# Where twenty-nine modulation tiles are read, and which engine makes the value blocks' low parts, in a two-layer diffusion backbone

## The reference, cut to what matters

```python
def even_project(u, w_in, ...):
    z = (u @ w_in).astype(jnp.float32)
    gq, gk, gv, gg, ga, mq, mk, mv, mo, mg = jnp.split(z, splits, axis=-1)
    ...
    if rope_gla is not None:                      # latent tokens only
        gq, gk = apply_rope(gq, *rope_gla), apply_rope(gk, *rope_gla)
        mq, mk = apply_rope(mq, *rope_ml), apply_rope(mk, *rope_ml)
    log_a = (jax.nn.log_sigmoid(a_pre) / GLA_TAU)...
    ...
def apply_rope(x, cos, sin):
    x1, x2 = x[..., :half], x[..., half:]
    return jnp.concatenate([x1 * c - x2 * s, x1 * s + x2 * c], axis=-1)
...
    m_lat = (jax.nn.silu(c) @ mod_w[layer] + mod_b[layer])[:, None, :]     # mod_w[layer]: 1024 x 6144
    sh1, sc1, g1, sh2, sc2, g2 = jnp.split(m_lat, 6, axis=-1)
```

## Time and profile before

| | |
|---|---|
| time, median of 3 runs | 1694.23 us (1692.0 to 1694.25) |
| the profiled execution's own time | 1690.38 us, of which the profile's span is 1688.6 us |
| TensorE matmuls busy | 1642.8 us, 97% of the span |
| VectorE / ScalarE / GpSimd busy | 1128.0 / 898.9 / 674.4 us |
| mean granted TensorE clock | 0.991 of full speed |
| weights loaded by SyncE | 281 transfers of 512 KB |

### The profile page before, as it was taken

One profiled execution on the slowest core, in us unless ns is written; L12 is line 12 of the kernel. 1 busy time (PEld: TensorE's weight loads), 2 busy tenths in 40 slices (PEclk: granted clock), 3 DMA queues, 4 the chain that ended last, 5 costly groups with the idle time before them and its releaser, 6 DMA issues.

```text
span 1688.6 us, 27407 instructions
## 1 busy us (share of the span) xinstructions
PE 1642.8 (97%) x10094; PEld 1451.7 (86%) x10094; DVE 1128.0 (67%) x1807; ACT 898.9 (53%) x1529; POOL 674.4 (40%) x494
## 2 busy tenths in 40 slices
PE   8999999998999999999999999999999999999997
PEld 5777888887899999999888889987668989998886
DVE  4678866667978888888657664145773778886113
ACT  5682435776565556665333453214883557776332
POOL 1233225453234444443443533342005266665444
PEclk9999999999999999999999999999999999999998
DMA  9423224343212223233733333364214123223221
GB/s 360 152 87 125 77 76 150 102 142 123 76 59 76 94 91 103 88 98 111 279 129 120 125 113 125 125 220 151 86 58 149 51 89 110 98 100 106 94 94 63
DMA packets 71240, 197.43 MB, mean 117 GB/s; under 512 B 6322, under 2 KB 27186, under 8 KB 69826
## 3 DMA queue, kind: packets, MB, share of 16 engines
q1 hardware_dynamic: 49268, 177.29, 30.1%
q10 hardware_dynamic: 21840, 18.40, 3.7%
HBM read 187.22 MB, written 8.45 MB: 116 GB/s over the span
## 4 chain that ended last, share of the span: by engine, by line
PE 68%; DVE 15%; ACT 5%; issue 2%; DMA 2%; POOL 2%; ACTq 0%; DVEq 0%; SPq 0%; POOLq 0%
PE ps L3824 19%; PE ps L3959 7%; PE ps L3319 6%; PE ps L4027 6%; PE ps L3446 5%; PE ps L3332 4%; PE ps L3956 3%; PE ps L3318 2%; PE ps L3774 2%; DMA raw<-in_weights 2%; PE ps L4127 2%; PE ps L4140 2%; PE ps L4106 2%; PE ps L3897 2%; PE ps L3452 1%
## 5 line engine op out<-in xcount | busy, mean ns | idle before, releaser
L895 POOL TENSOR_TENSOR wsp<-raw,wsp 128x512 fp32r<-128x512 f32 x220 | 326.6, 1505 | 691.4 <-ACT wsp L1048 691.0
L1048 ACT ACTIVATE wsp<-raw 128x1024 fp32r<-128x1024 f32 x110 | 116.7, 1061 | 169.5 <-PE ps L3319 84.2
L3959 PE MATMUL ps<-hsp,wsp 128*128 128x512 f32 x456 | 154.6, 391 | 0.0
L3824 PE MATMUL ps<-T,wun 128*128 128x384 f32 (+1 forms) x792 | 148.6, 340 | 3.9 <-DVE ps L2225 3.1
L3824 PEld LDWEIGHTS ps<-T,wun 128*128 128x128 f32 x792 | 141.4, 190 | 4.6 <-issue 4.5
L3332 PE MATMUL ps<-wsp,u 128*128 128x512 f32 x576 | 133.2, 391 | 2.6 <-POOL wsp L895 1.3
L3332 PEld LDWEIGHTS ps<-wsp,u 128*128 128x128 f32 x576 | 107.5, 188 | 28.0 <-POOL wsp L895 2.3
L3319 PE MATMUL ps<-u,wsp 128*128 128x512 f32 (+1 forms) x384 | 125.3, 362 | 0.0
L3446 PE MATMUL ps<-u,wsp 128*128 128x512 f32 x384 | 122.8, 402 | 0.0
L3956 PE MATMUL ps<-hsp,wsp 128*128 128x256 f32 x432 | 119.8, 281 | 2.6 <-DVE hsp L2821 2.1
L4027 PE MATMUL ps<-hsp,wsp 128*128 128x512 f32 x480 | 110.9, 390 | 1.8 <-POOL wsp L895 1.8
(11 more groups left out here) (412 smaller groups left out, 3866.8 us busy)
## 6 DMA issues: line engine op xcount, KB each, us to landing
raw<-in_weights SPq DMA_DIRECT2D x281, 512.0 KB, 3.3
nab<-in_nabias ACTq DMA_DIRECT2D x32, 256.0 KB, 2.7
start_w<-in_start SPq DMA_DIRECT2D x6, 1024.0 KB, 19.8
hidden_scratch<-hid0a SPq DMA_DIRECT2D x16, 384.0 KB, 4.7
hid0a<-hidden_scratch SPq DMA_DIRECT2D x5, 768.0 KB, 6.8
h<-in_x SPq DMA_DIRECT2D x4, 768.0 KB, 7.8
mD<-rows_scratch ACTq DMA_DIRECT2D x12, 256.0 KB, 3.9
mqs<-rows_scratch ACTq DMA_DIRECT2D x12, 256.0 KB, 4.8
```

Of the source, the lines that this page charges most:

```text
L895: pool.tensor_tensor(w[:, 1, half], raw[:, raw_index(s) % 4, half], w[:, 0, half].bitcast(F32), ALU.subtract)\
L1048: act.activation(split_of(s)[:, 0, :], raw[:, raw_s % 4, :], ACT.Copy).then_inc(*own.one(hi_ready))
L3824: mm = pe.matmul(out, UNIT[x][:, wp, tile(i)], operand[:, i, xp, 0:out.shape[-1]], start=(start and i == 0 and a == 0), stop=(i == KH - 1 ...
L3959: mm = pe.matmul(lat_of(layer, g, mm_), w, hsp[:, kk, xp, LAT], start=one, stop=last, skip_group_check=True)
```

## The change

Four modulation tiles leave the value blocks. After the change value blocks 5 to 8 have none, every later block up to 28 does a tile with a lower number than before, and blocks 22, 24, 26 and 28 (`TWO_MODS`) do two. The load order follows: w4, m4, w5, w6, w7, w8, w9, m5, w10, m6, w11, ... w20, m16, w21, m17, w22, m18, m19, w23, m20, w24, m21, m22, w25, m23, w26, m24, m25, w27, m26, w28, m27, m28, w29.

`value_low(b)` makes value block b's low part on VectorE, in one instruction over 1024 elements; GpSimd passes over those eight blocks. For n = 1 to 4 VectorE makes half of the rotated copy (two copies of 32 partitions), ScalarE the other half.

```diff
+TWO_MODS = [s_feat(n) for n in (14, 16, 18, 20)]
+def mods_of(s):
+    if S_V <= s < S_V + 4:
+        return []
+    first = s if s < S_V else s - 4 + sum(x < s for x in TWO_MODS)
+    return range(first, first + 1 + (s in TWO_MODS))
...
-        order += [("w", s)] + ([("m", MOD_FIRST + s)] if s < S_OUT0 else
+        order += [("w", s)] + ([("m", MOD_FIRST + x) for x in mods_of(s)] if s < S_OUT0 else
...
-            for s in range(N_START, s_feat(P2_FIRST) + 2):
+            for s in range(N_START, S_V):
+                low(s, 0)
+            lo_ready.k += N_V
+            pool.wait_ge(lo_ready.sem, s_count(S_V + N_V - 1, 0))
+            for s in range(S_V + N_V, s_feat(P2_FIRST) + 2):
                 low(s, 0)
...
-                    for a in range(0, P, half):
+                    mine = P // 2 if n <= 4 else P
+                    for a in range(0, mine, half):
...
             def modulate(s, i):
-                modulation(MOD_FIRST + s, c_both, left, (1, 0))
+                for x in mods_of(s) if s < S_OUT0 else (s,):
+                    modulation(MOD_FIRST + x, c_both, left, (1, 0))
...
+                for a in range(P // 2, P, half) if n <= 4 else ():
+                    dve.tensor_copy(xs[a:a + half, :], lat_bank(n)[a ^ half:(a ^ half) + half, :]).then_inc(*own.one(dve_own))
                 dve.wait_ge(in_act_took.sem, n + 1)
...
+            def value_low(b):
+                s = S_V + b
+                w = split_of(s)
+                dve.wait_ge(lo_ready.sem, s_count(s - 1, 0))
+                dve.wait_ge(hi_ready.sem, s_count(s, 0))
+                dve.tensor_tensor(w[:, 1, :], raw[:, raw_index(s) % 4, :], w[:, 0, :].bitcast(F32), ALU.subtract)\
+                   .then_inc(lo_ready.sem, 1)
...
             modulate(S_V, 0)
+            value_low(0)
             turned(4)
+            value_low(1)
             running_sum(0)
+            value_low(2)
             running_sum(1)
...
                     running_sum(3)
+                elif b in (1, 2):
+                    value_low(b + 2)
...
                     decayed(2)
+                    value_low(5)
                     decayed(3)
```

More of the change, by code:

```diff
@@ L92, with s_feat @@
 V_N = V_CCOL + 2 * KT
+def s_feat(n):
+    return n if n < N_FIRST else n + N_V
+TWO_MODS = [s_feat(n) for n in (14, 16, 18, 20)]
[4 more added lines that the diff above has]
+    return range(first, first + 1 + (s in TWO_MODS))
 def load_order():
@@ L118, in raw_index @@
     return PLACE["w", s]
-def s_feat(n):
-    return n if n < N_FIRST else n + N_V
 def steps_in(first, steps, slots, i):
@@ L1379, in evict @@
                         act.wait_ge(xs_used.sem, n - 1)
-                    for a in range(0, P, half):
+                    mine = P // 2 if n <= 4 else P
+                    for a in range(0, mine, half):
                         b = a ^ half
-                        last = a + half == P
+                        last = a + half == mine
                         act.activation(xs[a:a + half, :], lat[b:b + half, :], ACT.Copy)\
@@ L2383, in turned @@
                 cos, sin = (0, 1) if n <= 4 else (2, 3)
+                half = GLA_DK // 2
+                for a in range(P // 2, P, half) if n <= 4 else ():
+                    dve.tensor_copy(xs[a:a + half, :], lat_bank(n)[a ^ half:(a ^ half) + half, :]).then_inc(*own.one(dve_own))
                 dve.wait_ge(in_act_took.sem, n + 1)
@@ L2496, in _ @@
                     dve.memset(gS[:, :, 0, :, :], 0.0).then_inc(*own.one(state_zero))
+                    value_low(6)
                 if b == 5:
                     rows_sums()
+                    value_low(7)
                     rows_gains()
```

## The result

The changed kernel takes 1716.61 us (median of 4 runs, 1715.14 to 1717.86), the kernel before, on the same chip, 1693.49 us: ratio 1.014, 95% interval 1.0126 to 1.0154. The profiled execution took 1715.1 us, its span is 1713.2 (before: 1688.6).

A forecast was written before the change was run, and what follows sets the result against it. Bound: TensorE's work plus what keeps it waiting. 1690.4 - 3.4 (value blocks) + 22.8 (mLSTM waits) + 3 (clock) = 1712.8, with 3.8 to the median 1716 us; own range 1706 to 1724, widened for rivals to 1700 to 1726.

The forecast's parts named there:

- seven late loads: In mLSTM, w23 to w29 wait for slots freed only when ScalarE wants to split; 22.8 us of TensorE waits.
- The 3.8 us added for the median: Whole kernel: the median of runs lies 3.8 us above the profiled execution's 1690.4 us, so that is added.
- Value blocks: From 88 to 158 us, shorter waits and half the lost clock back: 3.4 us gained, bounds 1.5 and 6.
- The clock: After the value blocks, 1.7 us lost to the lower clock; half taken as regained, given a longer block 8 wait.
- Low part at its bare time: Value blocks: VectorE's low part takes 1.3 us with GpSimd idle; if contended, 2.0 us and 0.7 us less gain.
- Waits against clock: In mLSTM, 22.8 us of TensorE waits, plus 3 us for lower clock behind the four longer waits.
- Alone it would be hidden: In mLSTM, the moved tiles' 10 us of work on VectorE, two thirds busy, would by itself cost nothing.
- The 5.5 us for units 9 to 11: End of mLSTM: w29 about 2.5 us late, m28 a second tile, masking 0.3 us to spare; bounds 4 and 7.
- Loads in time: Rival, chance 0.08: mLSTM's loads arrive in time, only the value blocks change; gain 3.4 us, 1690.8 us.
- swallowed after the first pair: Rival, chance 0.11: in mLSTM, lateness beyond units 1 and 2 falls into ScalarE's idle times; 1700 us.
- TensorE is what counts: Rival, chance 0.04: whole kernel, no matmul changes, the 3.4 us gain and late loads about cancel; 1694 us.
- VectorE also bound in the value blocks: Rival, chance 0.11: copies cost 0.69 us, block 8's low part comes at 116; no gain there, more mLSTM contention; 1723 us.

The follow-up runs named there:

- Move_only: The kernel before with only the tiles moved and loads ordered as in the changed kernel; GpSimd keeps low parts, ScalarE whole copies: 1714.55 us, ratio 1.014.
- whole_copies: The changed kernel with all four rotated copies wholly on ScalarE again: one run, 1714.71 us.
- extra_work: The kernel before with two more multiplications of the same tile in blocks 22, 24, 26 and 28, loads as before: 1697.3 us, ratio 1.0033.
- order_ahead: The changed kernel with the weights of blocks 23 to 29 loaded one block further ahead: 1696.94 us, ratio 1.0026 to the kernel before.
- gla_same_order: The kernel before with only the tiles moved, doubled blocks 14, 16, 18, 20 in GLA, loads ordered as in the changed kernel: 1697.28 us, ratio 1.0035.
- value_only: The changed kernel with every tile back at its own block, VectorE keeping low parts and half copies: 1691.26 us, ratio 1.0002.

## Why the prediction was right, and where its terms were not

The predicted 1716 us is 0.6 from the measured 1716.61. The mechanism, seven late loads, was right; that the number is so close is luck. For the profiled execution the sum gave 1712.8 and it took 1715.1. The 3.8 us added for the median would have been 1.5 after the change, mLSTM cost 1.5 us more than the sum had, the value blocks gained 1.3 more, and 2 us behind mLSTM were in no term. The lower end of the forecast's own range, 1706, does not follow from its bounds either: 1716 less 2.6 for the gain and 5.7 for the waits is 1708.

- **Value blocks, 3.4 us forecast, 4.7 measured.** Up to block 8: 1.0 against 0.7, with a wait of 1.37 us where 2.1 was forecast, since the low part took 1.20 us and the scans before it came earlier. The prediction took 109.2 us as the time at which ScalarE's logarithms for them were there; VectorE was busy with a modulation until then, and ScalarE's two instructions, which start at 107.79 and take 1.58 in all, had the first half ready at about 108.6 (an estimate). After the change VectorE does wait for them, until 106.97. From there to 149 us: 0.6 against 0.5. The last copies: 1.6 against 1.3. The clock: 1.55, where I took 0.9, half of what was lost before. The wait at block 8 drew no dip, and that was the term most mis-sized. Move_only confirms where the last two come from, the modulations that no longer stand in front. The 0.5 us that the half copies were to give ahead of the value blocks lie within what the traces show (25.80 to 88.17 us: 0.1 to 0.7 gained in five kernels with them, between 0.2 gained and 0.4 lost in the seven without), but whole_copies and the changed kernel differ by 1.4 us up to 170 us. 1.2 us of that lie between 88 us and block 8, where I had expected nothing: with whole copies TensorE waits 0.6 us for the last rotation (`gqk`) and 1.7 at block 8, with half copies 1.4 at block 8 alone.
- **Low part at its bare time.** The low part took 1.20 us beside the 1.3 forecast. By the rule of the Trainium skill's GPSIMD Engine Reference, Specifications, that GpSimd shares its path to SBUF with VectorE and contends with VectorE's instructions that have two SBUF inputs, nothing is lost where GpSimd is idle, and the trace agrees: GpSimd does nothing from 84 to 148 us in the changed kernel. One row was misread, though: the scan of 1.76 us at 110.22 was not without GpSimd, whose low part starts at 110.66. The price is right even so: in the changed kernel the scans at 98.51, 102.28 and 107.96 us, GpSimd idle, take 1.76 too. In mLSTM the trace agrees with the rule as well: a multiplication at 286.85 us, GpSimd idle, took 1.22 us, and two at the end, beside GpSimd's four for the output, 2.27 and 2.29 (VectorE's timeline, then GpSimd's, changed kernel):

```profile
395.04 2.27 DVE L2085 SCALAR_TENSOR_TENSOR raw<-raw,c_both 128x1024 f32<-128x1024 f32 x1
...
399.48 2.29 DVE L2085 SCALAR_TENSOR_TENSOR raw<-raw,c_both 128x1024 f32<-128x1024 f32 x1
```

```profile
392.75 7.94 POOL L952 TENSOR_TENSOR u<-gt,u 128x512 fp32r<-128x512 f32 x4
```

- **Seven late loads.** All seven splits waited, in the seven units named, by 2.4 to 5.0 us. Unit 1 came 1.4 us late (forecast 1.5), unit 2 by 7.5 in all (7.8), the turn-back of unit 5 by 14.9 (13.9), the end of mLSTM by 27.3 (25.8, which is 22.8 and 3).
- **Waits against clock.** In 5 us stretches from 275 to 425 us TensorE's time without work rose from 7.7 to 25.4 us, 17.7 more, where 22.8 of waits were forecast. Its busy time lost to the lower clock (busy us times one less the granted clock, summed) rose from 1.4 to 9.8 us, 8.4 more, where I had 3. The forecast counted a unit's lateness as wait, while part of it was matmuls at the lower clock. It priced four dips at 1.5 us each and took two of them off, one as hidden and one as there before. The stretches show five, behind the waits at 290, 325, 353, 400 and 411 us, with 2.4, 2.0, 1.7, 2.3 and 1.4 us lost, and only the 1.4 us from before to take off. The two errors, 5.1 us too much and 5.4 too little, cancelled, which was luck.
- **"Alone it would be hidden"**, of the moved tiles' own work, is the step that failed. That work costs 7 us (extra_work) to 9 (order_ahead) in mLSTM, where it stands ahead of what TensorE waits for, `mC` and `u`. In the changed kernel the late loads leave little of it to be seen, but at the end it shows: the earlier trace rows have the last modulation as one tile; m27 and m28 behind each other occupy VectorE from 393.49 to 401.7, and TensorE waits 5.27 us for `u`. The 5.5 us for units 9 to 11 named m28 but the wrong wait, the masking. Against the start of mLSTM, the turn-back of unit 8 is 21.2 us late and the end 27.3, so 6.1 for the last units (5.5 forecast, 4 to 7) and 6.3 for units 6 to 8, where 3.4 and a part of the clock's 3 were forecast.
- **The rivals.** "Loads in time" fell with the seven splits; "swallowed after the first pair" fell with unit 5 in mLSTM; in GLA most late loads are swallowed (gla_same_order). "TensorE is what counts" would have been 1694: no matmul was touched and the time rose by 1.4%, since that engine was made to wait and to run slower. What the Trainium skill says in Perfetto Trace Analysis, Identifying the Most-Contended Engine, is to optimize that engine first; it does not say that a change elsewhere leaves the time alone, and no run here bears on it. "VectorE also bound in the value blocks" did not happen in the changed kernel; value_only comes nearest to it, and there nothing is gained as long as the modulations stay.

## What to carry to other kernels

A tile that moves takes a place in the queue of loads, and in a ring of buffers everything behind it can change its slot: work out for each later load what it now waits for, before costing the work that was moved. SyncE's order counts as well as the slot: a load that is free to go waits behind one that is not. The same four tiles cost 1.4% among mLSTM's short units and gain 0.2% among GLA's longer blocks with the loads a block ahead, and it took both: loads ahead alone left 0.3% lost (order_ahead), the place alone 0.35% (gla_same_order). A bundle of edits should be taken apart in both directions: here one of three carried most of the gain and all of the loss.

## What the runs showed of the hardware that was not expected

The granted clock can cost TensorE a good part of a wait again once the wait is over, and the extra grows less than the wait. The loss here is busy time times one less the granted clock, over the 5 us stretches of the dip. Behind waits of 1.86 us (changed kernel), 2.2 and 3.1 (before) and 3.87 (value_only) it is 1.4 to 1.7 us; behind 4.16, 5.27 and 6.76 us (changed kernel) and 5.7 (gla_same_order) it is 2.0 to 2.6. A wait of 1.37 us at block 8 drew no dip, but two of 0.95 and 1.06 us, 2 us apart, were followed in the changed kernel by 0.84 from 410 to 415 us and 0.81 from 415 to 420, 1.4 us lost.
